# Order of TensorE's work in one step of grouped-query attention

## The chip, the cores and the metric

The kernel runs on one core of a Trainium2 chip. The time is that of the device for one launch, in microseconds (us). Lower is better.

## The reference, cut to what matters

The program computes four layers on 1024 tokens of width 1024, all in float32: two recurrent layers, a neighbourhood attention with a mixture of experts, and a grouped-query attention with a mixture of experts. The change touches only the grouped-query attention, which has 16 query heads, 4 key and value heads and 64 elements a head:

```python
def one_block(qb):                      # 128 queries
    s = jnp.einsum('bqkgd,bskd->bkgqs', qb, k).astype(jnp.float32) * scale
    p = jax.nn.softmax(s, axis=-1).astype(v.dtype)
    return jnp.einsum('bkgqs,bskd->bqkgd', p, v)
```

## The kernel before, in words

`program` runs stages one after the other, each between barriers. The stage of the change is `grouped_query_stage` (line 1890). It walks over 4 key/value heads g. For each there are 16 steps: 2 pairs of query heads j, times 8 tiles t of 128 queries. That makes 64 steps (`count`), numbered i, with n = i mod 16. A step handles two heads, 128 queries each, against all 1024 keys. Its parts, with the letters used below:

- **S**, `scores` (line 1955): four matmuls of 512 columns into PSUM banks 0 to 3. The two heads use the two halves of the array's rows (64*128). S of step i waits until both exponentials of step i-1 have read these banks.
- VectorE, `find_top`: the row maximum of each head (line 2121). ScalarE, `exp`: exponential and row sum (line 2045). VectorE, `normalise`: reciprocal (2126) and product (2129).
- **T0** and **T1**, `turn(i, 0)` and `turn(i, 1)` (line 1968): eight transposes each, of one head's probabilities, four into bank 4 and four into bank 5. Both heads use the same two banks, so T1 waits for the copies of T0's banks. ScalarE copies bank 4 to SBUF (line 2039), VectorE copies bank 5 (line 2135).
- **W**, `weigh` (line 1979): the probabilities times the values, 16 matmuls of 128 columns, two heads side by side on the halves of the array's columns (128*64), into bank 6. W of step i waits for both heads' copies, and for `finish(i - 1)`, VectorE's copy of bank 6 (line 2140).
- **P**, `project` (line 1927): the query, key and value projections of the next g, cut into units that `advance` places behind T0 and T1. `GQA_UNITS` gives the counts: two and two for n = 0 to 7 (each pair is four matmuls of 384 columns, line 1940), one or none for n = 8 to 15 (four transposes, line 1950), and nothing for the last g. GpSimd does the rotary part of the next g (lines 2085 to 2100), after ScalarE's `take_root` at n = 4 and 8, which waits for VectorE's `sum_squares` (line 2116).

Every engine works through its own list in the order in which the code issues it. Nothing is planned by a cost model. TensorE's loop is lines 1995 to 2007: the body with number i holds S of i+1, T0 of i, W of i-1, T1 of i. ScalarE's body (2058 to 2075) is: copy of T0's bank 4, the two exponentials of i+1, copy of T1's bank 4, with the evictions of P before and after that copy. VectorE's body (2153 to 2167) is: two maxima of i+1, copy of T0's bank 5, normalise head 0 of i+1, copy of T1's bank 5, normalise head 1, `sum_squares` at n = 4 and 8, then `finish` of i-1. SyncE's weight loads wait only on the count of finished pieces of P.

Of the kernel before, what the change touches and what calls it, by code (L numbers as in the profile page):

```python
# [131 lines left out]
def ident(m, n=P):  # L132
    return m.const[0:n, K_IDENT:K_IDENT + n]
# [116 lines left out]
def advance(work, n):  # L250

    for _ in range(n):
        next(work, None)
# [1600 lines left out]
def first_bank(piece):  # L1854

    return 4 + piece if piece < GQA_BEGUN else piece - GQA_BEGUN if piece < NT else 7
# [33 lines left out]
def grouped_query_stage(nc, m, a):  # L1890
# [22 lines left out]
    with nc.Block() as block:  # L1913
        @block.sync
        def _(sp):
            sp.dma_start(gain_q, a["gqa_q_norm_2"][0].partition_broadcast(P)).then_inc(tables, 16)
            sp.dma_start(gain_k, a["gqa_k_norm_2"][0].partition_broadcast(P)).then_inc(tables, 16)
            sp.dma_start(rope, a["rope"].rearrange("(t p) n -> p t n", p=P)).then_inc(tables, 16)
            for g in range(1, KV_HEADS):
                sp.wait_ge(projected, GQA_PIECES * (g - 1) + NT - GQA_BEGUN)  # L1920
                load_group_weights(sp, a["gqa_w_qkv_2"][0], w, g, (loaded,) * 3)
            sp.wait_ge(projected, GQA_PIECES * (KV_HEADS - 1) + NT - GQA_BEGUN)
            load_out_weights(sp, m, a["gqa_w_o_2"][0], s["stored"])
            sp.wait_ge(s["stored"], 16 * (NK // 2))

        @block.tensor
        def _(pe):
            def project(g):
                for n in range(GQA_PIECES):
                    piece = GQA_PIECES * g + n  # L1930
                    if piece < GQA_BEGUN:
                        continue
                    bank = first_bank(piece)
                    if bank == 7:
                        pe.wait_ge(evicted, piece)
                    if n == 0:
                        pe.wait_ge(loaded, 48 * g)
                    if n < NT:
                        for k in range(NK):
                            last = pe.matmul(m.ps[:, bank, 0:WIDE], m.xT[:, k, n * P:(n + 1) * P], w[:, k, :],  # L1940
                                             start=(k == 0), stop=(k == NK - 1))
                            if k == NK - 1:
                                last.then_inc(projected, 1)
                            if k % 2 == 1:
                                yield
                    else:
                        half, j = divmod(n - NT, 3)
                        pe.wait_ge(roped, 2 * g + half + 1)
                        for t in range(half_tiles):
                            last = pe.transpose(m.ps[:, 7, t * P:(t + 1) * P],  # L1950
                                                raw[:, half * half_tiles + t, j * P:(j + 1) * P], ident(m))
                        last.then_inc(projected, 1)
                        yield

            def scores(i):
                g, j, t = i // 16, i // NT % 2, i % NT
                if i:
                    pe.wait_ge(exponent, 2 * i)
                if i % 16 == 0:
                    pe.wait_ge(evicted, GQA_PIECES * (g + 1))  # L1960
                for half in range(2):
                    for head in range(2):
                        d = slice(64 * head, 64 * head + 64)
                        last = pe.matmul(m.ps[:, 2 * head + half, :], q[g % 2][j][d, t * P:(t + 1) * P],  # L1964
                                         k2[g % 2][d, half * HALF:(half + 1) * HALF], start=True, stop=True)
                last.then_inc(scored, 1)

            def turn(i, head):
                pe.wait_ge(normalised, 2 * i + head + 1)
                for half, (copied, turned) in enumerate(((copied_4, turned_4), (copied_5, turned_5))):  # L1970
                    if 2 * i + head:
                        pe.wait_ge(copied, 2 * i + head)
                    for b in range(4):
                        last = pe.transpose(m.ps[:, 4 + half, b * P:(b + 1) * P],  # L1974
                                            prob[i % 2][head][:, half * HALF + b * P:half * HALF + (b + 1) * P],
                                            ident(m))
                    last.then_inc(turned, 1)

            def weigh(i):
                g = i // 16  # L1980
                pe.wait_ge(copied_4, 2 * i + 2)
                pe.wait_ge(copied_5, 2 * i + 2)
                pe.wait_ge(v_ready, 2 * (g + 1))
                if i:
                    pe.wait_ge(finished, i)
                for b in range(NT):
                    for head in range(2):
                        last = pe.matmul(m.ps[64 * head:64 * head + 64, 6, 0:P], v[g % 2][:, b, :],
                                         probT[i % 2][head][b // 4][:, b % 4 * P:(b % 4 + 1) * P], start=(b == 0), stop=(b == NT - 1))
                last.then_inc(weighed, 1)  # L1990

            for _ in project(0):
                pass
            scores(0)
            for i in range(count):
                g, n = divmod(i, 16)
                if n == 0:
                    work = project(g + 1) if g + 1 < KV_HEADS else iter(())
                if i + 1 < count:
                    scores(i + 1)  # L2000
                turn(i, 0)
                advance(work, GQA_UNITS[n][0])
                if i:
                    weigh(i - 1)
                turn(i, 1)
                advance(work, GQA_UNITS[n][1])
            weigh(count - 1)
# [1051 lines left out]
```

## Time and profile before

| | |
|---|---|
| median of 3 runs | 4433.46 us (4431.69 to 4436.14) |
| profiled execution, span from first to last instruction | 4435.6 us |
| of that, TensorE busy | 4032.6 us (91%) |
| VectorE, ScalarE, GpSimd busy | 2014.1, 1093.5, 511.2 us |
| grouped-query steps, first S to last W | about 3096 to 3622 us of the span |

The page states no other time for the profiled execution than its span, which is 2.1 us above the median of the runs. In the rows, a time of start is in microseconds from the start of the span. "PE" is TensorE's matmuls and transposes, "DVE" VectorE, "ACT" ScalarE, "POOL" GpSimd. A float32 matmul leaves two records, a transpose one. Matmuls are pipelined, so the step from one start to the next is what counts, not the duration.

### The profile page before, as it was taken

Reading aid. Unit: us, or ns where it says so; the run is one execution under the profiler, and the core shown is the slowest. Engines: PE = TensorE matmul, PEld = TensorE weight load, DVE = VectorE, ACT = ScalarE, POOL = GpSimd, SP = SyncE. Lnnn points to the kernel's source line nnn. Section 1 sums busy time; section 2 is a strip of 40 time slices with the busy share of each in tenths; the row PEclk is TensorE's granted clock in tenths of the full one; section 3 lists DMA queues with packets and bytes.
Section 4 is the critical chain, followed back from the end, with each engine's and each line's share of the span. In section 5 each row is a group of like instructions: output and inputs, shape, how many; then the busy total and the mean of one; then the engine's idle time right before and its main releaser. Section 6 shows DMA issues by size and latency. Waiting matters only on the chain. (4 is left out here: it accounts for less than half of the span.)

```text
span 4435.6 us, 81326 instructions
## 1 busy us (share of the span) xinstructions
PE 4032.6 (91%) x35518; PEld 2414.8 (54%) x35518; DVE 2014.1 (45%) x2992; ACT 1093.5 (25%) x1911; POOL 511.2 (12%) x348
## 2 busy tenths in 40 slices
PE   7999999899999998999896999866999998799973
PEld 3555664445556645566544666543666665465542
DVE  4555356456555554555554111005666776211104
ACT  2334223133431221222210000003444531000002
POOL 1232011032211100000000000000211300000001
PEclk9999999999999999999997999987999999899997
DMA  3332202323230244554424999982000122799996
GB/s 104 105 105 92 76 24 81 82 96 105 96 95 29 86 124 107 88 85 78 87 92 166 402 403 400 395 328 85 15 1 15 39 78 90 264 400 402 401 396 264
DMA packets 283516, 708.06 MB, mean 160 GB/s; under 512 B 57371, under 2 KB 183267, under 8 KB 266135
## 3 DMA queue, kind: packets, MB, share of 16 engines
q1 hardware_dynamic: 270471, 657.91, 42.7%
q0 software_dynamic: 11488, 40.64, 2.8%
q8 instruction: 286, 4.69, 0.4%
q10 hardware_dynamic: 1200, 4.24, 0.2%
q14 instruction: 71, 0.58, 0.0%
HBM read 630.51 MB, written 63.82 MB: 157 GB/s over the span
## 5 line engine op out<-in xcount | busy, mean ns | idle before, releaser
L493 PE MATMUL ps<-sb_mixT,sb_work 128*128 128x512 f32 x768 | 359.3, 604 | 9.6 <-ACT sb_x_tok L846 5.5
L493 PE MATMUL ps<-sb_xT,sb_work 128*128 128x512 f32 x768 | 359.1, 604 | 9.6 <-ACT sb_x_tok L846 5.5
L1634 PE MATMUL ps<-sb_xT,sb_work 128*128 128x512 f32 x512 | 236.2, 600 | 0.0
L493 PEld LDWEIGHTS ps<-sb_mixT,sb_work 128*128 128x128 f32 x768 | 138.0, 192 | 147.7 <-issue 129.8
L493 PEld LDWEIGHTS ps<-sb_xT,sb_work 128*128 128x128 f32 x768 | 138.0, 192 | 147.6 <-issue 129.7
L2615 PE MATMUL ps<-sb_work,sb_mixT 128*32 128x256 f32 x3264 | 191.8, 390 | 15.1 <-DMA sb_work<-moe_w_up 14.4
L2615 PE MATMUL ps<-sb_work,sb_xT 128*32 128x256 f32 x3264 | 188.8, 386 | 7.8 <-DMA sb_work<-moe_w_up 7.1
L2121 DVE TENSOR_REDUCE sb_cols<-ps 128x1 f32<-128x1024 f32 x128 | 150.7, 1219 | 85.9 <-PE ps L1964 85.8
L2682 ACT COPY sb_work<-ps 128x384 f32<-128x384 f32 (+2 forms) x66 | 29.7, 450 | 608.9 <-PE ps L2626 608.9
L2615 PE MATMUL ps<-sb_mixT,sb_xT 128*32 128x256 f32 x2496 | 150.9, 396 | 25.2 <-DMA sb_mixT<-moe_w_up 24.5
L2699 DVE TENSOR_TENSOR sb_work<-ps,sb_work 128x768 f32<-128x768 f32 (+2 forms) x66 | 58.4, 885 | 242.5 <-PE ps L2638 242.5
L2615 PE MATMUL ps<-sb_xT,sb_mixT 128*32 128x256 f32 x2496 | 147.7, 390 | 19.5 <-DMA sb_xT<-moe_w_up 18.9
L1940 PE MATMUL ps<-sb_work,sb_mixT 128*128 128x384 f32 x448 | 155.7, 494 | 4.1 <-PEq L93 4.1
L2615 PEld LDWEIGHTS ps<-sb_work,sb_mixT 128*32 128x32 f32 x3264 | 107.2, 113 | 88.1 <-issue 25.1
L2615 PEld LDWEIGHTS ps<-sb_work,sb_xT 128*32 128x32 f32 x3264 | 106.1, 111 | 78.9 <-issue 15.5
L1634 PEld LDWEIGHTS ps<-sb_xT,sb_work 128*128 128x128 f32 x512 | 91.0, 190 | 104.2 <-issue 104.2
L2045 ACT ACTIVATE sb_work<-ps,sb_cols 128x1024 f32<-128x1024 f32 x128 | 142.8, 1115 | 17.8 <-DVE sb_cols L2121 12.3
L1974 PEld LDWEIGHTS ps<-sb_const,sb_work 128*128 128x128 f32 x1024 | 109.8, 141 | 63.4 <-issue 32.9
L2693 DVE COPY sb_xT<-ps 128x384 f32<-128x384 f32 (+2 forms) x33 | 17.2, 522 | 279.0 <-PE ps L2602 279.0
L2693 DVE COPY sb_mixT<-ps 128x384 f32<-128x384 f32 (+2 forms) x33 | 17.2, 522 | 278.4 <-PE ps L2602 278.4
L1974 PE MATMUL ps<-sb_const,sb_work 128*128 128x128 f32 x1024 | 141.1, 280 | 1.9 <-DVE sb_work L2129 0.9
L2638 PE MATMUL ps<-sb_work 128*32 128x256 f32 x2496 | 140.7, 379 | 0.0
(489 smaller groups left out, 7338.6 us busy)
## 6 DMA issues: line engine op xcount, KB each, us to landing
sb_work<-moe_w_gate SPq DMA_DIRECT2D x34, 2048.0 KB, 8.3
sb_work<-moe_w_up SPq DMA_DIRECT2D x34, 2048.0 KB, 13.2
sb_work<-moe_w_down SPq DMA_DIRECT2D x32, 2048.0 KB, 19.7
sb_mixT<-moe_w_down SPq DMA_DIRECT2D x17, 2048.0 KB, 20.0
sb_xT<-moe_w_down SPq DMA_DIRECT2D x17, 2048.0 KB, 21.4
sb_xT<-moe_w_gate SPq DMA_DIRECT2D x16, 2048.0 KB, 8.0
sb_xT<-moe_w_up SPq DMA_DIRECT2D x16, 2048.0 KB, 12.7
sb_mixT<-moe_w_gate SPq DMA_DIRECT2D x16, 2048.0 KB, 8.1
```

The costliest lines, as they stand in the source:

```text
L493: last = pe.matmul(m.ps[:, bank, :], b.w[i][:, k, :], m.xT[:, k, half * HALF:(half + 1) * HALF], start=(k == 0), stop=(k == NK - 1))
L1634: last = pe.matmul(m.ps[:, bank, :], w[j // 2][:, k, :], m.xT[:, k, j % 2 * HALF:(j % 2 + 1) * HALF], start=(k == 0), stop=(k == NK - 1))
L1940: last = pe.matmul(m.ps[:, bank, 0:WIDE], m.xT[:, k, n * P:(n + 1) * P], w[:, k, :], start=(k == 0), stop=(k == NK - 1))
L1974: last = pe.transpose(m.ps[:, 4 + half, b * P:(b + 1) * P], prob[i % 2][head][:, half * HALF + b * P:half * HALF + (b + 1) * P], ident(m))
L2045: act.activation(prob[i % 2][head], banks(m, 2 * head), ACT.Exp, bias=top[:, column(i, head)], accum_out=total[:, column(i, head)]).then_i ...
L2121: dve.tensor_reduce(top[:, column(i, head)], banks(m, 2 * head), AX.X, ALU.max, negate=True).then_inc(found, 1)
L2615: last = pe.matmul(strip_sums(2 + 2 * (n % 2), tile[j])[:, g, :], b.x_turned[n % 2][:, k, g * STRIP:(g + 1) * STRIP], b.gate_up[n % 2][:, ...
L2638: last = pe.matmul(strip_sums(6, tile[j])[:, g, :], b.act_turned[n % 2][:, g, tile[k]], b.down[n % 2][:, k, j * 2 * P:(j + 1) * 2 * P], st ...
L2682: act.copy(b.act_turned[n % 2][:, 0:strips[n], :], chunks(m.ps[:, 0, :])[:, 0:strips[n], :]).then_inc(h_copied, 1)
L2693: dve.tensor_copy(b.x_turned[n % 2][:, 4:8, 0:rows], chunks(m.ps[:, 1, :])[:, :, 0:rows]).then_inc(x_copied, 1)
L2699: dve.tensor_tensor(b.y[n % 2][:, 0:strips[n], :], strip_sums(6)[:, 0:strips[n], :], each_chunk(b.gate_row, strips[n]), ALU.mult).then_inc ...
```

## The change

Three lines of TensorE's loop change places. `weigh(i - 1)`, with its waits, is issued ahead of `turn(i, 0)` instead of between it and `turn(i, 1)`. No instruction is added or removed, on any engine, and the lists of the other engines stay as they are.

```diff
                 if i + 1 < count:
                     scores(i + 1)
+                if i:
+                    weigh(i - 1)
                 turn(i, 0)
                 advance(work, GQA_UNITS[n][0])
-                if i:
-                    weigh(i - 1)
                 turn(i, 1)
                 advance(work, GQA_UNITS[n][1])
```

## Rows read from the trace of the kernel before

**Rows 1.** The page's busy line: busy time, share of the span, instructions.

```profile
PE 4032.6 (91%) x35518; PEld 2414.8 (54%) x35518; DVE 2014.1 (45%) x2992; ACT 1093.5 (25%) x1911; POOL 511.2 (12%) x348
```

**Rows 2.** Windows: stretch, its length, busy time by engine, granted clock, DMA.

```profile
3480.00:3608.00 128.00, 125.60 (x1198) 88.73 (x1194) 118.55 (x189) 74.79 (x134) 17.96 (x16) 1.00 0.05 19
```

**Rows 3.** Timeline, last g, no projection: start, duration, engine, line, operation [idle before].

```profile
3525.91 1.99 PE L1964 MATMUL ps<-sb_work 64*128 64x512 f32 x8
...
3602.10 1.99 PE L1964 MATMUL ps<-sb_work 64*128 64x512 f32 x8
...
3603.67 0.28 DVE L2140 COPY sb_xT<-ps 128x128 f32<-128x128 f32 x1
3604.01 1.09 PE L1974 MATMUL ps<-sb_const,sb_work 128*128 128x128 f32 x8
3604.13 2.36 DVE L2121 TENSOR_REDUCE sb_cols<-ps 128x1 f32<-128x1024 f32 x2 [0.18 <-PE ps L1964]
3604.71 0.58 ACT L2039 COPY sb_work<-ps 128x512 f32<-128x512 f32 x1 [2.35 <-PE ps L1974]
3605.04 1.97 PE L1988 MATMUL ps<-sb_work,sb_v_tok 128*64 128x128 f32 x32
3605.39 1.11 ACT L2045 ACTIVATE sb_work<-ps,sb_cols 128x1024 f32<-128x1024 f32 x1
3606.52 1.11 ACT L2045 ACTIVATE sb_work<-ps,sb_cols 128x1024 f32<-128x1024 f32 x1
3606.93 1.09 PE L1974 MATMUL ps<-sb_const,sb_work 128*128 128x128 f32 x8
3607.96 1.99 PE L1964 MATMUL ps<-sb_work 64*128 64x512 f32 x8
...
3619.88 0.29 PE L1988 MATMUL ps<-sb_work,sb_v_tok 128*64 128x128 f32 x1 [1.07 <-DVE sb_xT L2140]
```

**Rows 4.** Timeline at a body with projection: T1, the copy of its bank 5.

```profile
3262.78 1.09 PE L1974 MATMUL ps<-sb_const,sb_work 128*128 128x128 f32 x8
...
3263.91 0.69 DVE L2135 COPY sb_spare<-ps 128x512 f32<-128x512 f32 x1 [2.70 <-PE ps L1974]
```

**Rows 5.** Timeline of TensorE, neighbourhood stage: projection then weighing, projection then transposes.

```profile
2167.93 2.74 PE L1634 MATMUL ps<-sb_xT,sb_work 128*128 128x512 f32 x6
2170.62 0.88 PE L1691 MATMUL ps<-sb_work 128*64 128x128 f32 x12
...
2172.27 2.84 PE L1634 MATMUL ps<-sb_xT,sb_work 128*128 128x512 f32 x6
2174.95 0.82 PE L1674 MATMUL ps<-sb_const,sb_work 128*128 128x128 f32 x6
```

**Rows 6.** Timeline at the stage's start: second exponential of step 0, S of step 1.

```profile
3102.44 1.11 ACT L2045 ACTIVATE sb_work<-ps,sb_cols 128x1024 f32<-128x1024 f32 x1
...
3103.69 3.78 PE L1964 MATMUL ps<-sb_work 64*128 64x512 f32 x8 [3.69 <-ACT sb_work L2045]
```

**Rows 7.** Timeline, bodies n = 8 to 15 of the first g.

```profile
3191.76 1.99 PE L1964 MATMUL ps<-sb_work 64*128 64x512 f32 x8
...
3199.19 1.48 DVE L2116 TENSOR_REDUCE sb_cols<-sb_work 128x20 f32<-128x1280 f32 x1
...
3203.76 3.49 POOL L2087 TENSOR_TENSOR sb_work<-sb_work,sb_spare 128x1024 f32<-128x1024 f32 x2
3203.83 2.83 DVE L2129 TENSOR_SCALAR sb_work<-sb_work,sb_cols 128x1024 f32<-128x1024 f32 x1
...
3238.47 1.99 PE L1964 MATMUL ps<-sb_work 64*128 64x512 f32 x8 [0.77 <-ACT sb_work L2027]
...
3244.34 1.99 PE L1964 MATMUL ps<-sb_work 64*128 64x512 f32 x8
```

**Rows 8.** Windows around a fall of the granted clock in a recurrent stage.

```profile
1523.00:1528.00 5.00, 1.69 (x26) 1.31 (x23) 4.96 (x7) 0.99 (x2) 0.00 (x0) 0.93 1.03 409
1528.00:1537.00 9.00, 8.42 (x26) 1.57 (x28) 8.43 (x9) 3.22 (x6) 2.81 (x2) 0.50 0.68 273
```

## Prediction

> **What bounds the kernel now.** I read the busy line first: TensorE is busy 91% of the span and no other engine over 45% [rows 1]. The windows of the changed stage come next, since the average says nothing about it. In its last quarter TensorE is busy 125.6 of 128 us and VectorE 118.6 of 128, at a granted clock of 1.00, the 2.4 GHz level [rows 2]. Two engines are nearly full, so the timeline has to say which chain sets the pace.
>
> Take a body of the last g, which has no projection [rows 3]. From the start of S at 3602.10 it goes: T0 after 1.91 us, W after 2.94, T1 after 4.83, the next S after 5.86. TensorE has no idle stretch between them. Beside it runs a loop through three engines. The maxima start 2.03 us after S. ScalarE copies bank 4 at 2.61, 0.70 after T0's start, and then takes the exponentials at 3.29 and 4.42. The next S may start once the second exponential is done: where TensorE really waited for it (3.69 us idle), S started 1.25 us after the exponential's start [rows 6]. That would be 5.67 here, 0.19 before the S that came. So the two chains are almost level. The reader should see how little slack there is, and that in ScalarE's list the copy of T0's bank stands *ahead of* both exponentials. Today the copy ends at 3.19, just before the exponential could start anyway.
>
> From S at 3525.91 to S at 3607.96 there are 14 such bodies of 5.86 us [rows 3]. In each of the first three g, the bodies n = 8 to 15 take 52.58 us together (3191.76 to 3244.34) [rows 7]; those for n = 0 to 7 carry projection, 11.03 us each by my reading of their starts, with TensorE full.
>
> **The change part by part.** No instruction comes or goes, no DMA is moved, and SyncE's list waits on counts that the move leaves in the same order. W and its waits now stand ahead of T0. Behind W on TensorE's list are T0, T1 and, through them, the copies of both other engines.
>
> *The light bodies.* I put the new order together from the same rows, S at 0.
> - W starts at 1.91. This joint, S then W, does not occur in the trace. I take the 1.91 of S then T0, which is also a change of array tiling. The lowest bound is S without any joint, 1.71, an estimate: the six 512-column records of a projection take 2.69, so at most 0.45 each and 0.43 without the joint, and S's eight run two by two [rows 5]; the highest is 2.1, another step of 0.2 as between transposes and W.
> - T0 starts 1.89 later, at 3.80 (W to T1 now: 3605.04 to 3606.93) [rows 3].
> - ScalarE's copy starts 0.70 later, at 4.50, and lasts 0.58, to 5.08. The maximum of head 0 has been ready since about 3.25. The first exponential therefore waits for the copy: 5.08 in place of 3.29.
> - The second follows after 1.13 (3605.39 to 3606.52), at 6.21, and S after 1.25 more, at 7.46 [rows 3, 6].
>
> So a body goes from 5.86 to 7.46 us. I use 7.45, with bounds of 7.15 (both small joints low) and 7.7. The other chains fit below it. TensorE: T1's first half waits for ScalarE's copy (5.1). Its second half waits for VectorE's, which starts 1.13 after T0 [rows 4], at 4.93, and ends at 5.6. So T1 is over at about 6.1, and TensorE then idles until 7.45. VectorE: normalise at 6.35 to 7.3, copy of T1's bank to 8.0, normalise to 8.85, `finish` (0.28) to 9.15, which is 1.7 into the next body and 0.2 before the next W asks for it.
>
> The last g then costs 14 x (7.45 - 5.86) = +22.3 us.
>
> For n = 8 to 15 of the other g:
> - n = 8, 12, 13, 15: 7.45 each. Their one unit of P (four transposes, about 0.5 us) falls into TensorE's new idle time.
> - n = 9: at n = 8 `sum_squares` (1.48) stands ahead of `finish` in VectorE's list [rows 7]. `finish` ends at 3.1 into body 9, so W waits 1.2 us there: 8.65. Before, W came a turn later and was covered.
> - n = 10: GpSimd's rotary products hold VectorE's product up, which lasted 2.83 us beside GpSimd's 3.49 us pair [rows 7]. The collision stays, at another place. I estimate 8.95 for n = 10 and 7.65 for n = 11, each within 1.5 us.
> - n = 14: S of the next g needs the last eviction of P, today a wait of 0.77 [rows 7]. The eviction now follows exponentials and copy: 6.21 + 1.1 + 0.6 + 0.7, so 8.55.
>
> The sum is 4 x 7.45 + 8.65 + 8.95 + 7.65 + 8.55 = 63.6, against 52.58: +11.0 for each g, +33.1 for three.
>
> *The heavy bodies.* TensorE is the bound. Of its six joints, S to T0 and P to W go, S to W and P to T1 come. In the neighbourhood stage P to W took 2.69 us and P to transposes 2.68 [rows 5]. So only S to W is open, -0.2 to +0.2 in each of 23 bodies. The delays of ScalarE and VectorE (S would be possible at 7.45) stay hidden below 11 us. I take 0, with -5 and +5 as ends.
>
> *The end.* The last W started 11.92 us after the last S (3607.96 to 3619.88) [rows 3]. New: W of step 62 waits for `finish` (9.15), T0 at 11.05, VectorE's copy from 12.2 to 12.85, the rest of T1 and its copy to 14.2, W at 14.2: +2.3. The next stage begins behind a barrier, so nothing takes this back.
>
> Sum: 22.3 + 33.1 + 0 + 2.3 = +57.7 us, on the profiled span of 4435.6. The span stands 2.1 above the median of the runs, so on the median it is 4433.5 + 57.7 = **4491 us**. Its own range: 38 light bodies by -0.3 to +0.25 and the terms above, 4478 to 4504.
>
> **The rivals.**
>
> *The exponentials are not held, the drains count: faster.* Each change of tiling on TensorE seems to cost about 0.2 us (S is 1.71 of array time and takes 1.91). The new order has T0 and T1 side by side, which saves one such joint in 38 light bodies, 7.6 us. If S and W, both split tilings, also meet without one, 62 x 0.2 = 12.4 more: 4413 us. It decides only if the loop through the exponentials stays below 5.6 us. For it: TensorE is full now. Against it: ScalarE's list has the copy first, and the copy can't start before 3.80 + 0.70. Chance 0.04. The Trainium skill ("TensorEngine Tiling (Array Packing)", Key Properties) says that changing the tiling mode drains TensorE; by that rule the light body's TensorE work shrinks. The trace's 1.91 against 1.71 agrees, but the rule does not see the loop that takes over.
>
> *The copies hide.* If the exponentials kept their place, only T1's wait for VectorE's copy would bind: 4.93 + 0.68 + 0.45 + 0.2 = 6.3 a body, +0.45 x 38 = +17, and with W's wait at n = 9 and the end +6: 4456 us. The list speaks against it. Chance 0.06.
>
> *VectorE's lag feeds back.* W now needs `finish` with 0.2 us to spare. If normalise and copies lag a little more, each body grows by up to 0.5: +19, 4510 us. Chance 0.12.
>
> *The clock falls.* From W's end at 3.8 to the next S there are 3.65 us with only transposes and two gaps. In a recurrent stage, the granted clock fell from 1.00 to 0.50 (1.2 GHz) after 5.0 us in which TensorE was busy 1.69 us [rows 8]. The new stretch has 1.7 us busy in 3.65, denser and shorter. At the lower clock S lasts 3.78 in place of 1.99 [rows 3, 6]. With S slow in every light body, 38 x 1.8 = +68: 4559 us. Chance 0.10. The Trainium skill ("TensorE: Matmul & The Clock Gate", Part 4) says that transposes don't count as activity in the way matmuls do, which would make the stretch look idle. That a stretch of transposes alone lets the clock fall, no row here shows.
>
> **How the numbers follow.** Forecast 0.68, feedback 0.12, clock 0.10, hidden copies 0.06, faster 0.04. The range takes the forecast's own and most of the feedback case, with more room at both ends for the n = 9 to 14 estimates: 4466 to 4516. Clock and faster cases are left out. A measurement of this kernel tells a difference of about 0.2% (9 us) from none. Slower by more than that: 0.93. Within it: 0.04, the case in which both small effects cancel. Faster: 0.03.
>
> **What would show it.** In the profile after, in a light body of the last g: S to S 7.3 to 7.6 us; ScalarE's first exponential about 0.6 us behind the start of its copy and no longer waiting for the maximum; TensorE idle over 1 us before S, ended by the second exponential; T1's wait ended by a copy. TensorE's busy time is unchanged, so its share falls. Heavy bodies stay at 11.0. The forecast is wrong if the light bodies stay below 6.5, if the granted clock in the last g is under 0.95, or if the difference sits outside the stage.

## The result and the profile after

The changed kernel takes 4483.11 us (median of 4 runs, 4477.13 to 4488.62) against 4433.94 us (4 runs): +49.2 us. The ratio is 1.0109, with a 95% interval of 1.0094 to 1.0123. The forecast was 4491, within 4466 to 4516. The ratios in this text are the recorded ones, which differ from the quotient of the two medians by up to 0.0006. One run of the kernel before, of 8441.13 us at a mean granted clock of 0.55, is counted among the 17 named below but is in no ratio.

The page's busy line after. TensorE has as much to do as before [rows 1], in a span that is 51.1 us longer (4486.7 against 4435.6):

```profile
PE 4033.2 (90%) x35518; PEld 2416.0 (54%) x35518; DVE 2019.5 (45%) x2992; ACT 1084.0 (24%) x1911; POOL 507.9 (11%) x348
```

The windows of the stage after. The first row is the same stretch as in [rows 2], where TensorE was busy 125.60 of 128 us. The other three are single light bodies of the last g, each with the clock granted at 1.00:

```profile
3480.00:3608.00 128.00, 107.21 (x980) 74.05 (x976) 94.77 (x148) 58.02 (x108) 17.98 (x17) 1.00 0.09 34
...
3558.89:3566.24 7.35, 6.02 (x56) 4.11 (x57) 5.59 (x10) 3.26 (x7) 0.00 (x0) 1.00 0.01 2
3588.29:3595.64 7.35, 6.02 (x58) 4.11 (x58) 5.59 (x10) 3.27 (x7) 0.00 (x0) 1.00 0.00 1
3617.67:3625.02 7.35, 6.02 (x57) 4.11 (x57) 5.59 (x10) 3.27 (x7) 0.00 (x0) 1.00 0.00 0
```

The timeline of that last body, all engines, as in [rows 3]:

```profile
3617.67 1.99 PE L1964 MATMUL ps<-sb_work 64*128 64x512 f32 x8 [1.00 <-ACT sb_work L2045]
...
3618.88 0.28 DVE L2140 COPY sb_xT<-ps 128x128 f32<-128x128 f32 x1
...
3619.59 1.97 PE L1988 MATMUL ps<-sb_work,sb_v_tok 128*64 128x128 f32 x32
3619.71 2.36 DVE L2121 TENSOR_REDUCE sb_cols<-ps 128x1 f32<-128x1024 f32 x2 [0.54 <-PE ps L1964]
...
3621.49 1.09 PE L1974 MATMUL ps<-sb_const,sb_work 128*128 128x128 f32 x8
3622.18 0.58 ACT L2039 COPY sb_work<-ps 128x512 f32<-128x512 f32 x1 [4.08 <-PE ps L1974]
3622.62 0.69 DVE L2135 COPY sb_spare<-ps 128x512 f32<-128x512 f32 x1 [0.55 <-PE ps L1974]
3622.66 1.12 ACT L2045 ACTIVATE sb_work<-ps,sb_cols 128x1024 f32<-128x1024 f32 x1
...
3622.91 1.11 PE L1974 MATMUL ps<-sb_const,sb_work 128*128 128x128 f32 x8 [0.33 <-ACT sb_work L2039]
...
3623.76 1.11 ACT L2045 ACTIVATE sb_work<-ps,sb_cols 128x1024 f32<-128x1024 f32 x1
...
3625.02 1.99 PE L1964 MATMUL ps<-sb_work 64*128 64x512 f32 x8 [1.00 <-ACT sb_work L2045]
```

Read it along the loop. S starts, W 1.92 us later, T0 after 1.90 more. ScalarE sat idle for 4.08 us before its copy, although the first maximum had been ready since 3620.93, for its next entry was the copy of T0's bank. Copy 0.69 after T0, first exponential 0.48 after the copy's start, second 1.10 later, S 1.26 later. The sum is 7.35 us, where the old order took 5.86 [rows 3]. TensorE's idle time before S, 1.00 us, is ended by the second exponential.

The waits view of the stage shows both ends of the chain. Columns: who waited for whom, us in total, times, longest. The first pair stood at 152.7 us before:

```profile
ACT sb_work L2039 <- PE ps L1974: 251.7, 76, 5.1
...
PE ps L1964 <- ACT sb_work L2045: 34.8, 36, 3.7
```

From the starts of S in both traces, the account of the 51.1 us of span is:

| part | before | after | difference | forecast |
|---|---|---|---|---|
| last g, 14 light bodies | 14 x 5.86 | 14 x 7.35 | +20.8 | +22.3 |
| n = 8 to 15, three g | 52.58, 52.57, 52.57 | 62.14, 62.16, 62.15 | +28.7 | +33.1 |
| heavy bodies, from S of step 1 | 10.88, then 23 x 11.03 | 10.62, then 23 x 10.88 | -3.7 | 0 |
| last S to next stage's first matmul | 15.40 | 19.58 | +4.2 | +2.3 |
| sum | | | +50.0 | +57.7 |

The other 1.1 us lie ahead of and behind these parts, in work that is the same in both kernels. Whole runs of one kernel differ by more than that.

Two singular bodies and the end, from the timeline after. At n = 9, W waits for `finish`, which stands behind `sum_squares`. At n = 10, VectorE's product beside GpSimd's took 1.14 us, not 2.83 [rows 7]. At the end, W of step 62 waits 2.64 us for `finish`:

```profile
3199.63 1.48 DVE L2116 TENSOR_REDUCE sb_cols<-sb_work 128x20 f32<-128x1280 f32 x1
3201.02 0.28 DVE L2140 COPY sb_xT<-ps 128x128 f32<-128x128 f32 x1
...
3201.45 1.97 PE L1988 MATMUL ps<-sb_work,sb_v_tok 128*64 128x128 f32 x32 [1.04 <-DVE sb_xT L2140]
...
3204.19 3.50 POOL L2087 TENSOR_TENSOR sb_work<-sb_work,sb_spare 128x1024 f32<-128x1024 f32 x2
...
3205.96 1.14 DVE L2129 TENSOR_SCALAR sb_work<-sb_work,sb_cols 128x1024 f32<-128x1024 f32 x1
...
3663.39 2.78 PE L1988 MATMUL ps<-sb_work,sb_v_tok 128*64 128x128 f32 x32 [2.64 <-DVE sb_xT L2140]
```

### The profile page after: what moved, and what is told of

Read it like the earlier page. It is cut to its first block and busy times, and to the rows that moved or that the text cites. A ratio compares the mean times of both kernels' runs of the same rounds, so it can differ in the third digit from the quotient of the medians.

```text
span 4486.7 us, 81326 instructions
## 1 busy us (share of the span) xinstructions
PE 4033.2 (90%) x35518; PEld 2416.0 (54%) x35518; DVE 2019.5 (45%) x2992; ACT 1084.0 (24%) x1911; POOL 507.9 (11%) x348
## 5 line engine op out<-in xcount | busy, mean ns | idle before, releaser
L1964 PE MATMUL ps<-sb_work 64*128 64x512 f32 x512 | 130.5, 629 | 40.3 <-ACT sb_work L2045 34.8
```

## Experiments

Theory: W ahead of T0 delays T0, ScalarE's copy of T0's bank holds the exponentials behind it in the list, and they hold S. In every kernel below a body's length is the distance from one start of S to the next in its trace. A diff is against the changed kernel, unless it says otherwise.

### Which entry of ScalarE's list holds the loop

```diff
-                copy_out(i, 0)
                 if i + 1 < count:
                     exp(i + 1, 0)
+                copy_out(i, 0)
+                if i + 1 < count:
                     exp(i + 1, 1)
```

> The changed kernel, with ScalarE's first exponential of the next step issued ahead of its copy of T0's bank; TensorE's order stays. Theory (the copy in ScalarE's list holds the exponentials back, and through them the next S): the first exponential starts at 3.3 us after S in place of 4.3, the copy at 4.5, the second exponential at 5.0, so S to S in the light bodies of the last g is 6.25 to 6.35 us in place of 7.35. Over 38 light bodies this takes 35 to 40 us off: about 4445. Rival (W ahead of T0 costs by its own waits for finish and the copies, or by TensorE's own time): the body stays at 7.35 and the time at 4483.

Measured: 4451.74 us (5 runs), ratio to the kernel before 1.0040 (1.0027 to 1.0053), and light bodies of 6.38 us. The time is 31.4 us below the changed kernel's 4483.11, which the bodies account for: 14 x 0.97 in the last g, 3 x 5.97 in n = 8 to 15 (56.18 against 62.15), 31.5 in all. The 4445 expected took one microsecond for each of 38 bodies; n = 8, 12 and 14 gave 0.5 to 0.75, and n = 10 lost 0.4, for VectorE's product met GpSimd's instruction earlier (1.08 us after its start, not 1.77). The timeline of a body of the last g:

```profile
3572.07 1.99 PE L1964 MATMUL ps<-sb_work 64*128 64x512 f32 x8
...
3575.37 1.12 ACT L2045 ACTIVATE sb_work<-ps,sb_cols 128x1024 f32<-128x1024 f32 x1 [2.90 <-DVE sb_cols L2122]
...
3576.69 0.58 ACT L2039 COPY sb_work<-ps 128x512 f32<-128x512 f32 x1
...
3577.17 1.12 ACT L2045 ACTIVATE sb_work<-ps,sb_cols 128x1024 f32<-128x1024 f32 x1
3577.42 1.11 PE L1974 MATMUL ps<-sb_const,sb_work 128*128 128x128 f32 x8 [0.33 <-ACT sb_work L2039]
...
3578.46 1.99 PE L1964 MATMUL ps<-sb_work 64*128 64x512 f32 x8
```

TensorE's order is that of the changed kernel and W has the same waits; only ScalarE's list differs. The first exponential is back at 3.30 us after S, from 4.99 in the changed kernel (the 4.3 in the expectation is a slip), now released by the maximum. The theory holds, and the waits of W are not what costs. Two-thirds of the light body's loss of 1.49 comes back (0.97). The rest is T1: its wait for the copy puts its start at 5.35 us after S, and the next S stands right behind it on TensorE.

### Both exponentials ahead of the copy

```diff
-                copy_out(i, 0)
                 if i + 1 < count:
                     exp(i + 1, 0)
                     exp(i + 1, 1)
+                copy_out(i, 0)
```

> The changed kernel with both exponentials issued ahead of ScalarE's copy of T0's bank. Theory (TensorE's T1 needs that copy as much as S needs the exponentials): the copy starts at 5.55 us after S, T1 at 6.15, and S, behind T1 on TensorE, at 7.2: the light body is 7.15 to 7.3, nearly all the loss is back, and TensorE's long wait moves from before S to before T1. Rival (only the exponentials' place matters): 6.4 or below, as with one exponential ahead.

Measured in one run: 4476.90 us; light bodies of the last g 7.24 us. From S of step 1 to S of step 63 it takes 549.5 us, against 550.1 in the changed kernel. The timeline:

```profile
3593.64 1.99 PE L1964 MATMUL ps<-sb_work 64*128 64x512 f32 x8
...
3596.93 1.11 ACT L2045 ACTIVATE sb_work<-ps,sb_cols 128x1024 f32<-128x1024 f32 x1 [3.04 <-DVE sb_cols L2121]
...
3599.17 0.58 ACT L2039 COPY sb_work<-ps 128x512 f32<-128x512 f32 x1
...
3599.89 1.07 PE L1974 MATMUL ps<-sb_const,sb_work 128*128 128x128 f32 x8 [1.26 <-ACT sb_work L2039]
3600.88 1.56 PE L1964 MATMUL ps<-sb_work 64*128 64x512 f32 x6
```

As expected, TensorE's wait has moved from S to T1: 1.26 us for the copy, none before S. With T0 late, the copy and the two exponentials all stand between T0 and the next S, and none of the three places for the copy (ahead of, between or behind the exponentials) takes all three off that path.

### Half of the move

```diff
                 if i:
-                    weigh(i - 1)
+                    weigh(i - 1, range(NT // 2))
                 turn(i, 0)
                 advance(work, GQA_UNITS[n][0])
+                if i:
+                    weigh(i - 1, range(NT // 2, NT))
                 turn(i, 1)
```

`weigh` takes the range of its matmuls; its waits stand ahead of the first half. (Its own lines are left out here.)

> The changed kernel with half of W (8 of its 16 matmuls) ahead of T0 and the other half between T0 and T1. Theory (light body = start of T0 after S + a fixed loop of 0.69 + 0.48 + 1.10 + 1.26 = 3.54 us through copy, two exponentials and S's wait): half of W takes 0.86 us and a change of tiling 0.2, T0 starts at 2.97, S to S is 6.5 us. Rival A (TensorE's own time is the bound; two more changes of tiling than before): 5.86 + 0.35 = 6.2 us. Rival B (any part of W ahead of T0 brings W's waits and so the whole loss): 7.35. By theory the time is 4483 - 38 x 0.85 + about 4 for the heavy bodies' two more joints = 4455.

Measured: 4459.71 us (4 runs), ratio to before 1.0065 (1.0050 to 1.0081). Light bodies of the last g are 6.48 us, as the theory had them. The whole time lies 5 us above the 4455 expected, and the trace shows where: the light bodies gave back 30.4 us, not 32.3, and the heavy ones cost 8.2, not 4. These are 11.18 us, 0.30 above the changed kernel's, and the first one 11.93, 1.3 above, begun at the 1.2 GHz level. The timeline:

```profile
3574.05 1.99 PE L1964 MATMUL ps<-sb_work 64*128 64x512 f32 x8 [0.39 <-ACT sb_work L2049]
...
3576.99 1.09 PE L1974 MATMUL ps<-sb_const,sb_work 128*128 128x128 f32 x8
...
3577.68 0.59 ACT L2043 COPY sb_work<-ps 128x512 f32<-128x512 f32 x1 [3.21 <-PE ps L1974]
...
3580.53 1.99 PE L1964 MATMUL ps<-sb_work 64*128 64x512 f32 x8 [0.40 <-ACT sb_work L2049]
```

T0 starts 2.94 us after S, and the next S 3.54 after T0, nearly the 3.53 of the changed kernel (3621.49 to 3625.02). So with half of W moved and with all of it, a light body is the start of T0 plus 3.54. With T0 at 1.91, as before, this would be 5.45. That lies below the 5.67 of the loop through the maximum and below TensorE's own 5.86, which is why the copy's place in the list did not show.

### The two halves of the step list apart

```diff
+                heavy = g + 1 < KV_HEADS and n < 8
-                if i:
+                if i and heavy:
                     weigh(i - 1)
                 turn(i, 0)
                 advance(work, GQA_UNITS[n][0])
+                if i and not heavy:
+                    weigh(i - 1)
                 turn(i, 1)
```

> W ahead of T0 only in the heavy bodies (n below 8, g below 3), the old order in all light ones. Theory (loss and gain are separate: the heavy bodies are bound by TensorE and save one change of tiling, 0.15 us in each): heavy bodies 10.88, light bodies 5.86, time 24 x 0.15 = 3.6 us below the kernel before, 4430.3, a ratio of 0.9992. Rival (the 0.15 comes from the light bodies' new slack, which lets copies run ahead): heavy bodies stay at 11.03 and the time does not move.

The complement has the two conditions exchanged:

> W ahead of T0 only in the light bodies, the old order in the heavy ones (the other half of the change). Theory (the two halves add up): heavy bodies 11.03 us, light ones as in the changed kernel (7.35 in the last g, 62.1 for n = 8 to 15 of a g), the time about 3.7 us above the changed kernel's. Rival (heavy and light bodies lean on each other through the copies that run ahead): the light bodies right behind the heavy ones differ from 7.35.

Measured for heavy bodies only: 4432.49 us (11 runs) against 4433.40 (16 runs), ratio 0.9996 (0.9987 to 1.0005). The time does not tell it from no change. The trace does: 21 of the 24 heavy bodies are 10.88 us, and the light ones are as before (5.86 in the last g). The first heavy body is 11.98, begun at the 1.2 GHz level, and the first of the next two g are 10.97 and 10.96. So from S of step 1 to S of step 63 the gain is 2.2 us (504.3 to 502.1), not the 3.6 expected.

Measured for light bodies only, in one run: 4483.12 us, heavy bodies 11.03, and the light bodies right behind them 7.35, 8.46, 8.07 as in the changed kernel. Its whole time does not show the 3.7 us that were expected above the changed kernel's, and one run can't; from S of step 1 to S of step 63 the trace has 553.6 against 550.1 us. Loss and gain are separate.

Where the 0.15 us comes from: TensorE's timeline of a heavy body after, and below it the projection and W before.

```profile
3278.78 1.09 PE L1974 MATMUL ps<-sb_const,sb_work 128*128 128x128 f32 x8
3279.71 2.75 PE L1940 MATMUL ps<-sb_work,sb_mixT 128*128 128x384 f32 x8
3282.29 1.04 PE L1974 MATMUL ps<-sb_const,sb_work 128*128 128x128 f32 x8
3283.16 2.75 PE L1940 MATMUL ps<-sb_work,sb_mixT 128*128 128x384 f32 x8
3285.84 1.56 PE L1964 MATMUL ps<-sb_work 64*128 64x512 f32 x6
```

```profile
3280.26 2.75 PE L1940 MATMUL ps<-sb_work,sb_mixT 128*128 128x384 f32 x8
3282.94 1.97 PE L1988 MATMUL ps<-sb_work,sb_v_tok 128*64 128x128 f32 x32
```

Projection to T1 takes 2.58 us and T1 to projection 0.87. Before, projection to W took 2.68 (3280.26 to 3282.94) and T1 to projection 0.93 (3284.84 to 3285.77). Here, transposes on the undivided array (128*128) behind a projection start 0.10 us sooner than W on the divided one, and the projection behind them starts 0.06 sooner. Whether the change of tiling costs this, or the kind of operation, no run here tells.

### `finish` ahead of `sum_squares`

```diff
-                if g + 1 < KV_HEADS and n in GQA_ROOTS:
-                    sum_squares(g + 1, GQA_ROOTS.index(n))
                 if i:
                     finish(i - 1)
+                if g + 1 < KV_HEADS and n in GQA_ROOTS:
+                    sum_squares(g + 1, GQA_ROOTS.index(n))
```

> The changed kernel with VectorE's finish issued ahead of sum_squares at n = 4 and 8. Theory (at n = 9 W waits for finish, which stands behind sum_squares): the body n = 9 takes 7.35 in place of 8.46 us, the others stay, 3 us in all. Rival (n = 9 is long for GpSimd's rotary work or the late root): it stays at 8.4.

Measured in one run: 4477.38 us. The body n = 9 is 7.35 us in all three g, as expected. But "the others stay" was wrong: n = 10 grew from 8.07 to 10.98, 10.99 and 9.37, so from S of step 1 to S of step 63 the stage is longer than the changed kernel's (553.0 against 550.1 us). The one run's whole time lies within the spread of the changed kernel's runs (4477.13 to 4488.62 us) and tells nothing. The timeline of all engines from body 9 on, and two windows:

```profile
3192.70 3.48 POOL L2087 TENSOR_TENSOR sb_work<-sb_work,sb_spare 128x1024 f32<-128x1024 f32 x2
3193.15 2.45 DVE L2129 TENSOR_SCALAR sb_work<-sb_work,sb_cols 128x1024 f32<-128x1024 f32 x1
...
3194.07 1.99 PE L1964 MATMUL ps<-sb_work 64*128 64x512 f32 x8 [0.89 <-ACT sb_work L2045]
...
3197.58 0.28 DVE L2140 COPY sb_xT<-ps 128x128 f32<-128x128 f32 x1
```

```profile
3196.50:3198.00 1.50, 0.00 (x0) 0.03 (x1) 1.50 (x3) 0.00 (x0) 1.50 (x2) 1.00 0.00 0
3199.00:3202.00 3.00, 3.00 (x26) 2.67 (x23) 1.12 (x1) 0.00 (x0) 2.77 (x5) 0.50 0.00 0
```

With body 9 shorter, VectorE's product runs into GpSimd's long instruction 0.45 us after that one starts, not 1.77 after. It is held for 1.7 us, `finish` comes late, and TensorE idles 1.95 us before W. Behind that gap the granted clock drops to the 1.2 GHz level for 3 us in the first two g. In the third it stays at 1.00 behind the same gap, and the body is 9.37: some 1.6 us of the other two bodies are the clock's. The wait removed was partly a cover for another one.

### GpSimd's long product cut in four

This is the kernel with W ahead of T0 in heavy bodies only, and this in `rotate`:

```diff
-                st.settle(engine.tensor_tensor(mine[:, :, of, :], mine[:, :, of, :], gain.unsqueeze(1).unsqueeze(
-                    1).to_broadcast([P, half_tiles, n, HD]), ALU.mult))
+                for t in range(half_tiles):
+                    last = engine.tensor_tensor(mine[:, t, of, :], mine[:, t, of, :],
+                                                gain.unsqueeze(1).to_broadcast([P, n, HD]), ALU.mult)
+                st.settle(last)
```

> W ahead of T0 in the heavy bodies only, and GpSimd's products with the gain cut into four instructions each. Theory (VectorE's product waits for one whole GpSimd instruction, 2.15 us of it in three traces): the product at n = 10 takes at most 1.6 us in place of 2.83, the body n = 10 goes from 8.46 to about 7.3, 3.5 us in all, and with the 3.6 of the heavy bodies the time is 4426 to 4427, a ratio of 0.9984. Rival (VectorE waits for the whole run of GpSimd's work, or loses the same in small pieces): the body n = 10 stays at 8.4.

Measured: 4422.48 us (12 runs) against 4434.82 (17 runs), ratio 0.9978 (0.9970 to 0.9987). It beats both kernels. From S of step 1 to S of step 63 the trace has 7.8 us less than before (496.5 against 504.3), which lies inside the interval of the ratio (5.8 to 13.3 us). The body n = 10 is 6.57, 6.57 and 6.56 us in place of 8.46, shorter than the 7.3 expected. The timeline:

```profile
3196.97 4.92 POOL L2091 TENSOR_TENSOR sb_work<-sb_work,sb_spare 128x256 f32<-128x256 f32 x8
3197.05 1.20 DVE L2134 TENSOR_SCALAR sb_work<-sb_work,sb_cols 128x1024 f32<-128x1024 f32 x1
3197.64 1.99 PE L1964 MATMUL ps<-sb_work 64*128 64x512 f32 x8
...
3204.21 1.99 PE L1964 MATMUL ps<-sb_work 64*128 64x512 f32 x8
```

GpSimd's work itself grew from 3.49 to 4.92 us; what ran later met other instructions, and n = 12 went from 6.30 to 6.44. VectorE's product fell from 2.83 to 1.20 us.

## Why the prediction was right, step by step

**The light body.** Forecast 7.45, measured 7.35, by the chain named: T0 at 3.80 (3.82), copy at 4.50 (4.51), first exponential at 5.08 (4.99), second at 6.21 (6.09), S at 7.45 (7.35). The 0.1 is the copy: I took its whole 0.58 before the next entry could start, and it took 0.48. S to W, which no row of before showed, took 1.92. The experiments with half the move and with one or both exponentials ahead of the copy show that this chain is the cause.

**n = 8 to 15.** +28.7 against +33.1. W's wait behind `sum_squares` was there: 1.04 us, body 8.46 (8.65 forecast). n = 14 is 8.40 (8.55, though the terms written there add up to 8.61), and S waits 1.62 us for the eviction of P. Of the 1.5 us too much in each g, 0.8 are the same 0.1 in each of eight bodies. The mis-sized term is n = 10, 8.95 forecast and 8.07 measured, partly given back at n = 11 (7.81, not 7.65). The forecast gave the collision 1.5 us there. The product was held for only 0.4, since VectorE got there 1.77 us into an instruction that holds it off for about 2.15.

**The heavy bodies.** Forecast 0 with ends at -5 and +5, measured -3.7, of which 0.26 is the first body. S to W was 1.92 like S to T0, so the one joint held open cost nothing. The gain came from a joint that the forecast had put at nothing. I looked at the right joints, but misread the row. In [rows 5], projection to transposes took 2.68, as projection to weighing did, and I took the two joints as equal. The duration column tells them apart: that projection block lasted 2.84 us, the other 2.74. So the transposes started 0.16 us before the end of their projection, weighing only 0.05 before the end of its own. The block of 2.84 follows matmuls on a divided array (64*128, line 1661), the other transposes on the undivided one. That its extra 0.1 is a joint at its front fits the 2.58 us measured here, but is argued, not tested.

**The end.** +4.2 against +2.3. W of step 62 started 8.98 us after S (9.15 forecast). What I left out is the clock: behind the gap of 2.64 us it was granted at 0.50, and W took 2.71 us to T0 in place of 1.90. The kernel with `finish` ahead settles the size: it has the same order there and the same gap of 2.64, the clock stayed at 1.00, and the end took 17.97 us in place of 19.58. That is +2.6, close to the forecast, and the clock cost the other 1.6. The windows of the changed kernel:

```profile
3661.00:3663.00 2.00, 0.00 (x0) 0.00 (x0) 1.97 (x5) 1.18 (x3) 0.00 (x0) 1.00 0.00 0
...
3665.00:3667.00 2.00, 2.00 (x16) 1.67 (x13) 0.00 (x0) 0.00 (x0) 0.00 (x0) 0.50 0.00 0
```

and the window behind the same gap in the kernel with `finish` ahead:

```profile
3654.00:3660.00 6.00, 4.10 (x48) 3.45 (x48) 2.01 (x5) 1.17 (x2) 0.00 (x0) 1.00 0.01 3
```

**The rivals.** *Faster*: a change of tiling is saved in the heavy bodies, 0.15 us each, but nothing shows of it in the light ones, where the loop is longer than TensorE's work. The 1.71 us for S without a joint was an estimate, and no run here measured it; the change of tiling whose removal could be measured gave 0.15 us, not 0.2, and S to W is no shorter than S to T0. The Trainium skill ("TensorEngine Tiling (Array Packing)", Key Properties) says that changing the mode drains the engine; the trace fits it where TensorE is the bound, 2.58 against 2.68 us. *The copies hide*: this fell, for ScalarE's wait for T0 grew from 152.7 to 251.7 us, and S waited for the exponential. With one exponential ahead, it is close to what is left: 6.38 us against the 6.3 worked out for it, though T1 waits there for ScalarE's copy and not for VectorE's. *VectorE's lag feeds back*: not in the light bodies, where `finish` ends 1.49 us after S and W starts at 1.92. *The clock falls*: not in the light bodies, 1.00 in all three windows, though 3.5 us pass between W's end and S with only transposes and gaps of 0.33 and 1.00. That rival's support was the Trainium skill ("TensorE: Matmul & The Clock Gate", Part 4), which says that a transpose doesn't count as TensorE being busy in the same way. In these bodies the clock stayed at 1.00 all the same.

## What to carry to other kernels

A move on a busy engine is priced by the loop it lengthens, not by the work it leaves unchanged: write down for each engine what stands behind the moved piece in *its* list. Here 1.90 us of delay for T0 cost 1.49 a body, because a copy stood ahead of two exponentials that did not need it. Before a wait is removed, look at what the later work will then meet; a body made 1.1 us shorter let the next one run into a GpSimd instruction, which lost 1.3 us, and 2.9 where the clock fell too. In a stage whose steps have different bounds, one order need not be the best for all of them.

## What the runs showed of the hardware

VectorE's product of 128x1024 in SBUF takes 0.75 us alone. Issued while one long GpSimd product runs (2.36 us, the first of the pair of 3.49), it is held off. Starting 0.07, 0.45, 0.90, 1.08, 1.53, 1.77 and 2.00 us after GpSimd's, it ended 2.90 to 2.92 us after GpSimd's start each time, in five traces (before, `finish` ahead, half of W, one exponential ahead, the changed kernel). Taking off its own 0.75 leaves 2.15. Where it started at 2.18, it took 0.75. So it is held until shortly before that one instruction ends, not for the whole run of them. Cutting the GpSimd instruction into four brought the product to 1.20 us.

The granted clock can drop behind a single gap, but need not. Idle stretches of 1.95 us (two of three, `finish` ahead) and of 2.64 us (the changed kernel, light bodies only) were each followed by some 3 us at 0.50. The third gap of 1.95 and the same gap of 2.64 in the kernel with `finish` ahead left the clock at 1.00. So did gaps of 1.93 to 2.04 us at the ends of three other kernels, and the regular gaps of 0.33 and 1.00 us in bodies of 7.35 us. No run here shows what decides between them.
